# One inference step of a hybrid diffusion layer on one core: the prompt chunk's 128 weighted rows are fetched and summed in another place

## The chip, the core and the metric

The kernel runs on one core of a Trainium2 chip. The core has a matrix engine (TensorE, PE in the profile), VectorE (DVE), ScalarE (ACT), GpSimd (POOL), a queue engine (SyncE, SP) and 16 DMA engines that serve all queues. The metric is the device time of one execution in microseconds, lower is better.

## The reference

Everything is float32. The layer takes 128 prompt tokens and 512 latent tokens (1024 features each) and computes, for both with the same weights: conditioning, normalisation, one input projection, windowed attention with 8 heads, a two-way linear recurrence, an output projection, and then the expert mixer PEER, which this change is about:

```python
def chunk(x):                                   # 128 tokens at a time, 5 chunks: 1 prompt, 4 latent
    q = (x @ w_q).reshape(128, 8, 2, 128)
    s = jnp.einsum('chpd,hpnd->chpn', q, sub_keys)
    st, it = lax.top_k(s, 16)
    cand = st[:, :, 0, :, None] + st[:, :, 1, None, :]
    cidx = it[:, :, 0, :, None] * 128 + it[:, :, 1, None, :]
    best, pos = lax.top_k(cand.reshape(128, 8, -1), 16)
    eidx = take_along_axis(cidx, pos)           # 8 heads x 16 = 128 experts per token
    g = jax.nn.softmax(best, axis=-1)
    act = jax.nn.gelu(einsum('chkd,cd->chk', u_tab[eidx], x))
    return einsum('chk,chkd->cd', g * act, v_tab[eidx])
```

The tables u_tab and v_tab have 16384 rows of 1024 numbers. The result is scaled by a gate, added to x, and x is normalised a last time.

## The kernel before, in words

The five chunks of 128 tokens are called 0 (the prompt), C1, C1+1, C3 and C4 (the latent ones). A token sits on a partition, so that expert slot k of a chunk is one "row": an indirect DMA on POOL's queue fetches, for each of the 128 partitions, the 4 KB row that `eidx[:, c, k]` names, 512 KB in all. A chunk has 128 u rows (each multiplied with x and summed to one dot product) and 128 v rows (each multiplied with a weight of the token, `gw[:, c, k]`, and summed over k).

The program goes through a front for the prompt (phase 0), the same for the latent tokens (phase 1), and then the work on rows.

**The front of phase 1.** The recurrence, then attention in eight quads (4 blocks of tokens times 2 kv heads, each with 4 heads), then the merge: for each of 8 output blocks m a gate product "ga" and an output product "ao" on PE, tanh on ACT, two products on DVE (L1608, L1609), then the output projection "mix" in four token blocks t, each followed by a normalisation on DVE (L1703, L1704) and transposes on PE. PE does the four blocks of mix in order and the transposes of block t after the product of block t+1. Last comes the product with w_q and the top-k of C1.

**The prompt's rows.** Calls `serve(n)` on DVE stand all through the front of phase 1. Each call takes the next n rows of chunk 0: first 128 u rows (L1357), and, once their gelu is done at the end of the recurrence stage (`gelu_dots(0)`), 128 v rows (L1366, one 128x1024 multiply-add into one of two accumulators). They are fetched by POOL into a ring of five buffers. In phase 1 the v rows stand so: 6 a quad in attention (`serve(4)` and `serve(2)`), 16 after it, 6 after each block m of the merge, 8 in each of the first two blocks t of mix; then `add_sums(0)` adds them to x.

**The latent rows.** The list `turns` gives the order in which POOL fetches rows and which engine takes each: step 0 the u rows of C1, step 1 those of C1+1, step 2 those of C3, step 3 the u rows of C4 and the v rows of C3 in turn, step 4 the v rows of C4. The rows share a ring; until step 2 it has 10 buffers (6 until turn 36), and a fetch takes the buffer that has been held longest, so that fetch n waits until row n-10 is used. Turn 36 waits for the end of the w_q product. DVE takes rows with `rows(n)` (L1384), between pieces of the routing of the next chunk: `route(c, piece)` has 12 pieces, eight with two top-k and a top-16 of sums, four that turn positions into expert numbers. `step_end` does the gelu of a chunk's dots.

**The dense chunks.** The v part of C1 and C1+1 is not fetched by rows: the weights are spread into a matrix over all 16384 experts. DVE makes one-hot tiles (`one_hots(i, m)`, L1760 and L1761, 8 instructions for a build of four tokens), PE multiplies them (L946), ACT moves the result (two copies a build), 32 builds for each of the two chunks. The 32 builds of C1 stand in step 1 beside the routing of C3; those of C1+1 follow it. `one_hots` waits for the build two before it (`w_full`). Then the dense product (L959) goes through the whole v table in 128 tiles of 512 KB, loaded by SP into five buffers.

**Summing rows on PE.** Half of the last v rows of C4 are summed by PE: ACT writes a 128x128 diagonal of the row's weights (four buffers), and PE multiplies it with the row, two products of 128x512 accumulated in two PSUM banks (L973; the trace shows four instructions a row).

The profile puts ACT's instructions all at one helper line (L996). DVE's marks go through helper lines too, which is why some waits end at "DVEq L1266".

## Time and profile before

| | us |
|---|---|
| median of 3 runs | 2691.29 (2688.75 to 2694.09) |
| the profiled execution, whole | 2691.56 |
| its span in the profile | 2689.8 |
| PE / DVE / POOL / ACT busy in the span | 1697.5 / 2003.3 / 1044.5 / 352.5 |
| moved by DMA | 753.39 MB, mean 280 GB/s |

All rows below are of the profiled execution. It is 1.8 us longer than its span. A busy share is an average over stages which have different limits, so the rows are mostly read stage by stage.

### The profile page before, as it was taken

How to read it: one execution, taken by the hardware profiler on the slowest of the kernel's cores; microseconds unless marked ns; L12 is line 12 of the kernel's file. 1: busy time of each engine (PE TensorE's matmuls, PEld its weight loads, DVE VectorE, ACT ScalarE, POOL GpSimd, SP SyncE). 2: the span in 40 equal slices, each digit the busy share in tenths (PEclk: the TensorE clock that was granted, in tenths of full speed). 3: DMA queues.
4: the chain of work that ended last, by engine and by line, in shares of the span. 5: the costliest groups of instructions: out<-in, count | busy, mean ns of one | idle time of the engine just before them, and what ended most of it. 6: DMA issues, size and time to landing. Idle time of an engine off the chain costs nothing.

```text
span 2689.8 us, 19725 instructions
## 1 busy us (share of the span) xinstructions
PE 1697.5 (63%) x5821; PEld 1075.7 (40%) x5821; DVE 2003.3 (74%) x4233; ACT 352.5 (13%) x811; POOL 1044.5 (39%) x1028
## 2 busy tenths in 40 slices
PE   6789668989877897794000332069999999000176
PEld 2568543444336545552000222066666666000032
DVE  1331486987679778488999999998876566998845
ACT  0451202541004200111000011020000000000111
POOL 0000002325635556022544343524435445777664
PEclk9899788999988998897555555569999999555588
DMA  9667545658966798263876767849999999999997
GB/s 291 193 203 234 169 151 165 218 180 308 348 203 207 245 374 289 81 219 127 306 283 234 252 224 239 318 157 348 411 410 407 409 409 409 410 370 378 361 373 291
DMA packets 296870, 753.39 MB, mean 280 GB/s; under 512 B 21502, under 2 KB 141102, under 8 KB 296244
## 3 DMA queue, kind: packets, MB, share of 16 engines
q0 software_dynamic: 147456, 536.94, 54.5%
q1 hardware_dynamic: 149308, 215.20, 22.8%
q8 instruction: 47, 0.77, 0.1%
q14 instruction: 59, 0.48, 0.1%
HBM read 740.72 MB, written 11.33 MB: 280 GB/s over the span
## 4 chain that ended last, share of the span: by engine, by line
DVE 41%; issue 26%; PE 16%; DMA 9%; ACT 3%; POOL 2%; DVEq 1%; SPq 0%; ACTq 0%; POOLq 0%
DVE attn L1384 6%; PE bank L724 4%; PE pair L724 4%; DVE big L1384 4%; PE bank L973 3%; DVE ring_more L1384 3%; DVE work L1760 3%; ACT work L996 2%; DMA h_all<-in_peer_u_dram,eidx 2%; DVE gf_row L1761 2%; DMA attn<-in_peer_u_dram,eidx 2%; DMA ring_more<-in_peer_v_dram,eidx 2%; DMA ring_more<-in_peer_u_dram,eidx 2%; PE bank L708 1%; DMA h_all<-in_peer_v_dram,eidx 1%
## 5 line engine op out<-in xcount | busy, mean ns | idle before, releaser
L724 PE MATMUL pair<-big 128*128 128x128 f32 (+1 forms) x1280 | 372.4, 450 | 36.4 <-DVEq L1266 24.9
L1842 POOL DMA_INDIRECT attn<-in_peer_u_dram,eidx x225 | 216.3, 961 | 389.1 <-DVE dots L1384 254.7
L1842 POOL DMA_INDIRECT h_all<-in_peer_u_dram,eidx x106 | 121.1, 1142 | 592.1 <-DVEq L1736 418.3
L724 PE MATMUL bank<-big 128*128 128x512 f32 (+1 forms) x1056 | 313.9, 459 | 37.3 <-DVEq L1270 17.8
L1384 DVE CUSTOM_DVE_ANT_0 attn<-attn,pair 128x1024 f32<-128x1024 f32 x225 | 267.4, 1218 | 45.1 <-DMA attn<-in_peer_u_dram,eidx 28.0
L724 PEld LDWEIGHTS pair<-big 128*128 128x128 f32 x1280 | 203.6, 201 | 192.5 <-issue 176.8
L959 PE MATMUL bank<-h_all,big 128*128 128x512 f32 x608 | 270.3, 601 | 9.9 <-DMA h_all<-in_peer_v_dram 9.2
L1842 POOL DMA_INDIRECT ring_more<-in_peer_u_dram,eidx x161 | 163.8, 1017 | 211.1 <-DVE dots L1384 121.8
L724 PEld LDWEIGHTS bank<-big 128*128 128x128 f32 x1056 | 173.5, 206 | 172.8 <-issue 163.0
L946 PE MATMUL bank<-work,gf_row 128*128 128x128 f32 x512 | 118.9, 409 | 163.4 <-DVE gf_row L1761 163.4
L973 PE MATMUL bank<-big,work 128*128 128x512 f32 x76 | 43.2, 708 | 281.9 <-ACT work L996 264.3
L959 PEld LDWEIGHTS bank<-h_all,big 128*128 128x128 f32 x608 | 180.6, 297 | 95.3 <-DMA h_all<-in_peer_v_dram 10.6
L937 PE MATMUL bank<-ident,sel 128*128 128x128 f32 x4 | 1.3, 439 | 299.5 <-DVEq L1749 299.5
L959 PE MATMUL bank<-big 128*128 128x512 f32 x416 | 182.8, 592 | 0.0
L946 PEld LDWEIGHTS bank<-work,gf_row 128*128 128x128 f32 x512 | 103.5, 300 | 179.1 <-DVE gf_row L1761 178.9
L1842 POOL DMA_INDIRECT big<-in_peer_u_dram,eidx x108 | 104.2, 965 | 109.2 <-DVE dots L1384 79.8
L959 PEld LDWEIGHTS bank<-big 128*128 128x128 f32 x416 | 123.5, 297 | 55.1
L1384 DVE CUSTOM_DVE_ANT_0 ring_more<-ring_more,pair 128x1024 f32<-128x1024 f32 x111 | 132.8, 1217 | 12.7 <-DMA ring_more<-in_peer_u_dram,eidx 8.5
L1842 POOL DMA_INDIRECT h_all<-in_peer_v_dram,eidx x94 | 107.1, 1140 | 85.9 <-DVE gf_row L1366 35.4
L973 PEld LDWEIGHTS bank<-big,work 128*128 128x128 f32 x76 | 16.3, 223 | 305.7 <-issue 305.7
L1384 DVE CUSTOM_DVE_ANT_0 big<-big,pair 128x1024 f32<-128x1024 f32 x108 | 127.4, 1216 | 8.4 <-DMA big<-in_peer_u_dram,eidx 8.1
L1842 POOL DMA_INDIRECT ring_more<-in_peer_v_dram,eidx x87 | 94.7, 1088 | 90.0 <-DVE gf_row L1366 40.4
(255 smaller groups left out, 2966.8 us busy)
## 6 DMA issues: line engine op xcount, KB each, us to landing
big<-in_w_in_dram SPq DMA_DIRECT2D x44, 1024.0 KB, 6.5
h_all<-in_peer_v_dram SPq DMA_DIRECT2D x76, 512.0 KB
big<-in_peer_v_dram SPq DMA_DIRECT2D x52, 512.0 KB
big<-in_w_ada_dram SPq DMA_DIRECT2D x24, 1024.0 KB, 5.5
big<-in_peer_w_q_dram SPq DMA_DIRECT2D x16, 1024.0 KB, 5.5
big<-in_w_rnn_o_dram SPq DMA_DIRECT2D x8, 1024.0 KB, 8.6
big<-in_w_attn_o_dram SPq DMA_DIRECT2D x8, 1024.0 KB, 7.5
big<-in_w_out_dram SPq DMA_DIRECT2D x8, 1024.0 KB, 11.9
```

The source lines that it names most:

```text
L708: last = nc.tensor.matmul(u[0:2, 0:TC], cond[:, k, :], w[:, k, :], start=(k == 0), stop=(k == KD - 1))
L724: last = nc.tensor.matmul(u[:, 0:n], w[:, k, col:col + P], src[:, k, 0:n], start=(k == 0), stop=(k == KD - 1))
L937: last = nc.tensor.transpose(psum[0][:, n * P:(n + 1) * P], src, ident[:, :])
L946: last = nc.tensor.matmul(psum[2 + b % 2][:, t * P:(t + 1) * P], hot_b[at], hot_a[at], start=True, stop=True)
L959: last = nc.tensor.matmul(psum[2 * (c % 2) + h][:, :], dense_w[c][:, q % 2, :, n % QI], v_tile[r][:, h * 512:(h + 1) * 512], start=(n == 0 ...
L973: last = nc.tensor.matmul(psum[i][:, :], diag[:, (n - 1) % DIAGS, :], ring[r][:, i * 512:(i + 1) * 512], start=(k == first_by_tensor), sto ...
L996: return nc.scalar.activation(out, in_, func, **kw)
L1384: V.tensor_tensor_reduce(ring[r], ring[r], x_at[c][:, :], 1.0, 0.0, ALU.mult, ALU.add, dots[:, k:k + 1]).then_inc(row_used["vector"], 1)
L1760: V.tensor_scalar(hot_a[t % HOTS], iota128[:, :], hi[:, t:t + 1], weight[:, t:t + 1], ALU.is_equal, ALU.mult)
L1761: last = V.tensor_scalar(hot_b[t % HOTS], iota128[:, :], lo[:, t:t + 1], None, ALU.is_equal)
L1842: g.indirect_dma_start(dst, None, ins["peer_" + table][0], bass.IndirectOffsetOnAxis(ap=eidx[:, c, k:k + 1], axis=0)).then_inc(landed, 16)
```

## The change

The 128 v rows of chunk 0 leave `serve` and with it the front of phase 1. They become turns of the list: 64 of them stand in step 0 among the u rows of C1 (after the first 36, in the places between 92 u rows), 64 in step 1, one after each two u rows of C1+1. All 128 are summed on PE with diagonals from ACT, into PSUM banks 0 and 1; the transposes of the expert numbers go to bank 2. POOL fetches them through the shared ring. DVE's code for them is gone; a new `add_prompt`, four instructions of 128x512, adds the sum to x in the middle of the builds of C1+1, and the last normalisation of chunk 0 (`final(0)`) follows the last of these builds instead of the end of step 0. On PE the builds of C1 and the weighted rows stand in one order, and so do the diagonals and the moves on ACT. The one-hot tiles use another buffer. The dense product's buffers are dealt out anew: two tiles are loaded ahead instead of three, and the store of chunk 0's result moves behind the load of tile 10.

```diff
     STAGE = 16
     QI = NKEY // 4
-    V_SLOTS, V_FIRST = 5, 3
+    V_SLOTS, V_FIRST = 5, 2
     ALONE = 24
-    turns = [(*step[n % len(step)], n // len(step)) for step in steps for n in range(len(step) * SLOTS)]
-    step_start = [sum(len(step) for step in steps[:i]) * SLOTS for i in range(len(steps))]
+    steps[0] = [("u", C1, k) for k in range(EARLY)]
+    half = SLOTS // 2
+    for k in range(SLOTS - EARLY):
+        n0, n1 = (j * half // (SLOTS - EARLY) for j in (k, k + 1))
+        steps[0] += [("u", C1, EARLY + k)] + [("v", 0, n) for n in range(n0, n1)]
+    steps[1] = []
+    for k in range(half):
+        steps[1] += [("u", C1 + 1, 2 * k), ("u", C1 + 1, 2 * k + 1), ("v", 0, half + k)]
+    steps[2:] = [[(*step[n % len(step)], n // len(step)) for n in range(len(step) * SLOTS)] for step in steps[2:]]
+    turns = [turn for step in steps for turn in step]
+    step_start = [sum(len(step) for step in steps[:i]) for i in range(len(steps))]
+    SOFT_LAG = 22
+    diffs_at = EARLY_ROWS * (2 * PH - 2) + (step_start[1] - EARLY_ROWS * (2 * PH - 2)) * PH // PIECES
+    hots_at = [step_start[1] + len(steps[1]) * PH // PIECES * m // BUILDS for m in range(BUILDS)]
+    later_diffs_at = step_start[1] + len(steps[1]) * PH // PIECES
     taken = {"vector": 0, "tensor": 0}
     by, count_after = [], []
     for table, c, k in turns:
-        by.append("tensor" if table == "v" and c == C4 and k >= ALONE and k % 2 == 0 else "vector")
+        by.append("tensor" if table == "v" and (c == 0 or c == C4 and k >= ALONE and k % 2 == 0) else "vector")
         taken[by[-1]] += 1
         count_after.append(taken[by[-1]])
...
-        acc0 = [gf_row[:, 1, :], final_row[:, :]]
...
-        v_tile = [h2_all[:, C1 + 1, :]] + [big[:, o_h + i * D:o_h + (i + 1) * D] for i in range(2)]
-        v_tile += [h2_all[:, i, :] for i in range(2)]
+        v_tile = [big[:, o_h + i * D:o_h + (i + 1) * D] for i in range(2)] + [h2_all[:, i, :] for i in range(3)]
...
-        hot_b = [gf_row[:, 0, t * P:(t + 1) * P] for t in range(HOTS)]
+        hot_b = [h2_all[:, C1 + 1, t * P:(t + 1) * P] for t in range(HOTS)]
...
-            store(0)
...
-            sp_.wait_ge(x_ready, 2 * len(DENSE))
...
+                if n == 2 * V_SLOTS:
+                    store(0)
...
+            next_row = [0]
+            def weighted_rows(end):
+                for turn in range(next_row[0], end):
+                    table, c, k = turns[turn]
+                    if by[turn] != "tensor":
+                        continue
+                    r, n = slot_of[turn], count_after[turn]
+                    pe.wait_ge(diag_ready, n)
+                    pe.wait_ge(row_in[r], landings[turn])
+                    for i in range(2):
+                        last = nc.tensor.matmul(psum[i][:, :], diag[:, (n - 1) % DIAGS, :],
+                                                ring[r][:, i * 512:(i + 1) * 512], start=(k == first_by_tensor[c]),
+                                                stop=(k == last_by_tensor[c]))
+                    last.then_inc(row_used["tensor"], 1)
+                next_row[0] = max(next_row[0], end)
...
+            def turn_ids(i):
                 pe.wait_ge(ids_split, i + 1)
...
+            weighted_rows(step_start[1])
+            turn_ids(0)
+            for m in range(BUILDS):
+                weighted_rows(hots_at[m])
+                weights(0, m)
+            weighted_rows(step_start[2])
+            pe.drain().then_inc(sums_full, 1)
+            pe.wait_ge(w_moved, BUILDS)
+            turn_ids(1)
+            for m in range(BUILDS):
+                weights(1, m)
+            pe.wait_ge(sums_free, 1)
...
-            pe.wait_ge(sums_free, 1)
...
+            pe.wait_ge(sums_free, 2)
+            weighted_rows(len(turns))
...
             soft(C1)
             spread_x(C1 + 1)
+            diags(diffs_at + SOFT_LAG)
             soft(C1 + 1)
+            diags(step_start[1])
             gelu_dots(C1)
-            final(0)
             spread_x(C3)
             spread_ids(0)
-            move_weights(0)
+            for m in range(BUILDS):
+                diags(hots_at[m])
+                move_weights(0, m)
+            diags(later_diffs_at + SOFT_LAG)
             soft(C3)
+            diags(step_start[2])
             gelu_dots(C1 + 1)
...
+            for m in range(BUILDS):
+                move_weights(1, m)
+            final(0)
...
-                    if s_ is None or s_ == 2 * SLOTS or (s_ == SLOTS and not gelu0[0]):
+                    if s_ is None or s_ == SLOTS:
...
-                    if s_ < SLOTS:
-                        V.tensor_tensor_reduce(ring0[r], ring0[r], h2_all[:, 0, :], 1.0, 0.0, ALU.mult, ALU.add,
-                                               dots[:, s_:s_ + 1]).then_inc(slot0_used, 1)
-                    else:
-                        a_, w_ = acc0[s_ % 2], gw[:, 0, s_ - SLOTS:s_ - SLOTS + 1]
-                        if s_ < SLOTS + 2:
-                            V.tensor_scalar(a_, ring0[r], w_, None, ALU.mult).then_inc(slot0_used, 1)
-                        else:
-                            dve.wait_ge(slot0_used, RING0 + s_ - 1)
-                            V.scalar_tensor_tensor(a_, ring0[r], w_, a_, ALU.mult, ALU.add).then_inc(slot0_used, 1)
+                    V.tensor_tensor_reduce(ring0[r], ring0[r], h2_all[:, 0, :], 1.0, 0.0, ALU.mult, ALU.add,
+                                           dots[:, s_:s_ + 1]).then_inc(slot0_used, 1)
...
                     if ph and t == 1:
-                        serve(2 * SLOTS)
-                        dve.wait_ge(slot0_used, RING0 + 2 * SLOTS)
-                        dve.wait_ge(final_in, 16)
-                        add_sums(0, acc0)
                         dve.drain().then_inc(sums0_done, 1)
...
+                    dve.wait_ge(x_ready, 2 * len(DENSE))
...
+            def add_prompt():
+                dve.wait_ge(sums_full, 1)
+                for i, h in enumerate([slice(i * 512, (i + 1) * 512) for i in range(2)]):
+                    link(V.tensor_tensor(psum[i][:, :], psum[i][:, :], gf_row[:, 0, h], ALU.mult))
+                    link(V.tensor_tensor(x_all[:, 0, h], x_all[:, 0, h], psum[i][:, :], ALU.add))
+                dve.drain().then_inc(sums_free, 1)
...
-            left = SLOTS - next_turn[0]
+            left = step_start[1] - next_turn[0]
             for piece in range(PIECES):
                 route(C1 + 1, piece)
                 rows(share(left, piece, PIECES))
             step_end(C1)
-            dve.wait_ge(final_in, 48)
-            final(0, hot[:, 0:D])
             split_ids(C1)
             for piece in range(PIECES):
                 route(C3, piece)
-                n_rows, n_hots = share(SLOTS, piece, PIECES), share(BUILDS, piece, PH) if piece < PH else 0
-                for m in range(n_hots):
-                    one_hots(0, BUILDS * piece // PH + m)
-                    rows(share(n_rows, m, n_hots))
-                if not n_hots:
-                    rows(n_rows)
+                for m in range(BUILDS * piece // PH, BUILDS * (piece + 1) // PH if piece < PH else 0):
+                    rows(hots_at[m] - next_turn[0])
+                    one_hots(0, m)
+                if piece >= PH:
+                    rows(max(later_diffs_at - next_turn[0], 0))
+                    rows(share(step_start[2] - later_diffs_at, piece - PH, PIECES - PH))
             step_end(C1 + 1)
             split_ids(C1 + 1)
             for m in range(BUILDS):
                 one_hots(1, m)
                 rows(m % 2)
+                if m == BUILDS // 2:
+                    add_prompt()
+            dve.wait_ge(final_in, 48)
+            final(0, hot[:, 0:D])
...
-            for n in range(2 * SLOTS):
+            for n in range(SLOTS):
                 r = n % RING0
                 pool.wait_ge(slot0_used, n + 1)
-                fetch("u" if n < SLOTS else "v", 0, n % SLOTS, ring0[r], row0_in[r])
-            pool.wait_ge(slot0_used, RING0 + 2 * SLOTS)
+                fetch("u", 0, n, ring0[r], row0_in[r])
+            pool.wait_ge(slot0_used, RING0 + SLOTS)
```

## Rows read from the trace of the kernel before

**Rows 1.** Busy time by stage: from:to, length, engines, granted PE clock, DMA share, GB/s
```profile
796.90:914.30 117.40, 87.10 (x502) 72.48 (x501) 101.91 (x133) 42.66 (x110) 55.26 (x46) 0.86 0.60 207
914.30:1036.40 122.10, 104.04 (x248) 46.03 (x246) 86.33 (x77) 7.25 (x11) 66.00 (x60) 0.95 0.92 334
1264.20:1455.30 191.10, 0.00 (x0) 0.00 (x0) 184.25 (x452) 0.43 (x2) 96.90 (x103) 0.50 0.77 276
1468.70:1669.10 200.40, 66.45 (x256) 57.03 (x256) 196.87 (x603) 22.02 (x65) 78.91 (x84) 0.50 0.69 232
1669.10:1747.70 78.60, 0.90 (x3) 0.50 (x3) 73.26 (x143) 1.86 (x7) 39.59 (x41) 0.50 0.85 307
1747.70:1824.20 76.50, 51.44 (x253) 45.74 (x254) 76.46 (x289) 20.41 (x63) 14.89 (x15) 0.70 0.51 162
1825.90:2280.10 454.20, 444.93 (x1024) 304.02 (x1024) 323.82 (x621) 1.95 (x6) 203.96 (x216) 0.99 1.02 406
1284.00:1300.00 16.00, 0.00 (x0) 0.00 (x0) 15.48 (x44) 0.00 (x0) 9.72 (x11) 0.50 1.03 414
```

**Rows 2.** The same by stage for line L1366 alone (DVE busy, clock, DMA)
```profile
796.90:914.30 117.40, 54.18 (x44) 0.86 0.60 207
914.30:1036.40 122.10, 75.31 (x60) 0.95 0.92 334
```

**Rows 3.** One attention quad: all engines' busy time, then PE and ACT instructions
```profile
816.60:831.60 15.00, 9.26 (x64) 8.63 (x63) 13.84 (x19) 5.90 (x14) 7.33 (x7) 0.81 0.61 217
831.60:845.40 13.80, 10.57 (x70) 9.83 (x70) 12.64 (x18) 5.25 (x14) 7.19 (x7) 0.87 0.64 220
...
828.98 1.97 PE L864 MATMUL pair<-ident,work 128*128 128x128 f32 x8 [5.74 <-DVEq L1266]
...
822.86 0.20 ACT L996 ACTIVATE q_es<-q_dif 128x4 f32<-128x4 f32 x1 [3.89 <-DVEq L1652]
```

**Rows 4.** PE in merge and mix (start, length, [idle before, releaser]); DVE's last merge
```profile
990.97 27.63 PE L724 MATMUL pair<-big 128*128 128x512 f32 x64
1036.44 30.17 PE L898 MATMUL bank<-big 128*128 128x256 f32 x128 [17.84 <-DVEq L1611]
...
1088.72 1.97 PE L890 MATMUL pair<-ident,h_all 128*128 128x128 f32 x8 [7.43 <-DVE h_all L1704]
...
1035.55 0.69 DVE L1609 TENSOR_TENSOR big<-big,work 128x512 f32<-128x512 f32 x1
```

**Rows 5.** A fetch and a product of u rows, POOL and DVE
```profile
1277.05 0.94 POOL L1842 DMA_INDIRECT big<-in_peer_u_dram,eidx  x1 [0.30 <-issue]
...
1453.87 1.22 DVE L1384 CUSTOM_DVE_ANT_0 big<-big,pair 128x1024 f32<-128x1024 f32 x1
```

**Rows 6.** Chain of waits: a u row on its way, start and length
```profile
1149.58 4.87 DMA attn<-in_peer_u_dram,eidx
```

**Rows 7.** A fetch beside one-hot tiles, POOL and DVE
```profile
1508.90 0.94 POOL L1842 DMA_INDIRECT ring_more<-in_peer_u_dram,eidx  x1 [0.30 <-issue]
...
1508.81 0.35 DVE L1760 TENSOR_SCALAR work<-vcols,attn 128x128 f32<-128x128 f32 x1
```

**Rows 8.** PE: weighted rows (four instructions each), then builds (eight each)
```profile
2554.00 1.88 PE L973 MATMUL bank<-h_all,work 128*128 128x512 f32 x4
...
2573.47 3.63 PE L973 MATMUL bank<-big,work 128*128 128x512 f32 x4 [2.15 <-issue]
...
1510.31 2.08 PE L946 MATMUL bank<-work,gf_row 128*128 128x128 f32 x8 [3.17 <-DVE gf_row L1761]
...
1797.46 1.16 PE L946 MATMUL bank<-work,gf_row 128*128 128x128 f32 x8 [1.81 <-DVE gf_row L1761]
```

**Rows 9.** ACT: one of a build's two moves
```profile
1507.18 0.38 ACT L996 ACTIVATE big<-bank 128x256 f32<-128x256 f32 x1 [4.60 <-PE bank L946]
```

**Rows 10.** DVE: first and last large instruction of final(0)
```profile
1457.01 1.23 DVE L1276 CUSTOM_DVE_ANT_0 work<-x_all 128x1024 f32<-128x1024 f32 x1 [0.18 <-DVE gw L1412]
...
1459.72 1.28 DVE L1426 SCALAR_TENSOR_TENSOR x_all<-x_all,nrm,final_row 128x1024 f32<-128x1024 f32 x1
```

80 lines of the change are left out of this document (33 added, 47 removed).

## The prediction

> **What bounds the kernel now.** I read the busy time by stage first, because 74% of busy DVE over the whole span says nothing of one stage. Four regimes are to be seen. In attention and merge of phase 1 DVE has most to do, 101.9 of 117.4 us, and then waits for rows, 86.3 of 122.1 us while the DMA share is 0.92 [rows 1]. In step 0 (1264 to 1455) and step 1 (1469 to 1748) DVE is busy 184.3 of 191.1, 196.9 of 200.4 and 73.3 of 78.6 us, with the DMA engines at 0.77, 0.69 and 0.85, PE at 0.50 of its clock and nearly idle [rows 1]. In the dense product PE is busy 444.9 of 454.2 us and the DMA engines are at 1.02, 406 GB/s [rows 1]. So the change takes work from a stretch that is bound by DVE and by its rows, and puts its fetches where DVE binds and the DMA engines have room; the room is what has to be counted. Second I read the line of the weighted rows by stage: 54.2 us of DVE in attention and 75.3 us up to the start of mix [rows 2]. Third the waits inside one quad, in merge and in mix.
>
> **The front.** 128 products of some 1.28 us leave DVE. What that is worth is the distance to what binds next.
> Attention: a quad takes 15.0 or 13.8 us, of which six v rows fill 7.4 to 7.7. PE then waits 5.74 us for a mark of DVE, ACT 3.89 us for the maxima [rows 3]. With the rows gone PE comes next: it is busy 9.3 and 10.6 us in the two quads [rows 3]. I take 10.0 us for a quad: 14.4 - 10.0 = 4.4, times 8 = 35 us, less 1 for the two ends, **-34**. Bounds: if only the row time that PE and ACT both wait for goes (3.9 of each quad in part, say 2) it is -16; if all of six rows goes, 7.5 x 8 = -60, which PE's busy time excludes below 9 us a quad, so -43.
> Merge and mix: PE ends its last merge products at 1018.6 (990.97 + 27.63) and starts mix at 1036.44, after 17.84 us of waiting for DVE's last merge, which ends at 1036.24 [rows 4]. Without six rows a block DVE needs two products of 0.7 us after PE's last one, so some 2 us stay: -16. In mix PE waits 7.43 us for the normalisation of block 1, behind `add_sums` and eight rows [rows 4]; without them DVE needs about 9.5 us a block where PE needs 15 (30.17 for two), so all of it goes: -7. Together **-23**. Here PE's own work cannot shrink, which makes this the surest term. The u part of chunk 0 stands before all this and stays. Front: -57.
>
> **Step 0.** DVE's own work stays at 191 us (rows of u, routing). The fetches grow: turns 38 to 191 are issued in it, 154 instead of 90, because ten are in the ring when the routing part before it ends. A fetch costs POOL 0.94 + 0.30 = 1.24 us back to back [rows 5]. In the stretch with fetches alone the DMA engines are at 1.03 and move 414 GB/s, that is 0.524 MB / 414 = 1.27 us a row [rows 1]. So 1.27 binds: the first issue comes with the first product at 1271, the last u row (turn 190) is issued 152 x 1.27 = 193 us later, at 1464, lands in 4.9 us [rows 6], more under load, say 6, and is multiplied in 1.22 [rows 5]: 1471 against 1455, +16. The queue is in order and a ring of 10 is short: in the 6 us of a routing piece 5 fetches fit, and 5 are on their way, so it holds just, and a v row keeps its buffer until ACT's diagonal and PE's product. I add 0.5 us in each of 12 pieces: **+22**. Bounds: 154 x 1.24 hidden up to landing, +8; 1.5 us a turn, 154 x 1.5 = 231, +47.
>
> **Step 1, beside the builds.** 16 turns a piece of 25.7 us (8 pieces, 206 us), 20.3 us of DMA: room. New is the order on PE and ACT: rows, build, two moves, the next diagonals, rows. A weighted row takes PE 1.88 us at the full clock and 3.63 after a pause of 2.15 us [rows 8], a build 1.16 or 2.08 [rows 8], the moves 2 x 0.38 [rows 9], diagonal and marks some 0.5. With 4/3 rows a build the cycle is 4.9 us at 2.4 GHz and 8.2 at 1.2 GHz, and DVE offers 206/32 = 6.4 and may lead by two builds only. In the builds of C1+1, PE is busy 67% of the time and granted 0.70 [rows 1]; the new mixture would be busy longer than that, so I take the same 0.70 at least: (1.16 + 2.5)/0.70 + 1.3 = 6.5 us, a tie, **+6** for bursts. Bounds 0 and (8.2 - 6.4) x 32 = +58.
> **Step 1, last four pieces**: 64 turns x 1.27 = 81 us against 73 of DVE work there; the ring is full at the start, which gives back part: **+5** (0 to +10).
> `final(0)` leaves the end of step 0: 1457.0 to 1461.0, **-4** [rows 10]. `step_end` waits for u rows alone; the last v row is 2 to 4 us later on PE and hidden by gelu, split and the first routing piece.
>
> **Builds of C1+1 and after.** DVE is busy 76.46 of 76.50 us there [rows 1], so `add_prompt` counts: four of 128x512, nearest row 0.69 [rows 4], with marks **+3**. `final(0)` comes after the last build, beside the dense product, where DVE has 130 us idle: 0 to +2. The third tile is no longer loaded ahead: two tiles last 2 x 3.5 us (454/128), a tile needs 4.9 or more [rows 6] from the last save on: +2. The store of chunk 0 (0.5 MB) now falls where the DMA engines are full: 0.524/406 = +1.3. Together **+4**. From here the fetches, their order and the bytes are those of before, and at 1.02 DMA share the rest moves as a whole.
>
> **Sum.** -34 - 23 + 22 + 6 + 5 - 4 + 3 + 4 = -21 us on the profiled execution's 2691.56 (span 2689.8 plus 1.8), which is 0.3 above the median shown: 2670.
>
> **Two rules of the Trainium skill against this.** A fetch beside one-hot tiles takes POOL 0.94 us, as any other, and the next follows after 0.30 [rows 7]. "SBUF — State Buffer", section "SBUF: two separate sides", says that a VectorE tensor_scalar can hold the port by which GpSimd writes its descriptors. By that rule the one-hots would shut POOL out for 8 x 0.3 us a build, and four fetches would need 5.0 + 2.4 = 7.4 us a build where 6.4 are there, +32; the trace does not show it, and I give it 3 in 100 (rival 4).
> After 2.15 us without work PE's next row is at the lower level [rows 8], and PE sits at 0.50 with 33% of busy time in step 1 today [rows 1]. "TensorE: Matmul & The Clock Gate", section "HAM oscillation — how this bites in real kernels", describes loops that wait for a DMA between short bursts and fall back each time. By that rule rows of both steps would start low; in step 0 this is harmless, a row every 3 x 1.27 = 3.8 us against 3.63; in step 1 it is rival 3.
>
> **Rivals.**
> 1. The room is there (20 in 100). Fetches run ahead, step 0 costs +8, step 1 nothing: -57 + 8 - 4 + 3 + 4 = -46, 2646. For it: DMA shares of 0.69 to 0.85. Against: 82 MB in step 0 at 414 GB/s is 198 us, more than DVE's 191.
> 2. The front gives less (13 in 100). ACT's exponentials and copies, which wait for PE in turn, make the quad 12.5 us instead of 10: -20 more away, 2690. For it: the three engines hand over some 20 times a quad; against: ACT is busy only 5.9 us [rows 3].
> 3. **Slower**: the chain of rows, build, moves and diagonals sets step 1 (14 in 100). PE stays at 1.2 GHz in it, 8.2 us a build, +58 instead of +6: -21 + 52 = +31, 2722. It decides from where a build takes 6.4 + (6 + 21)/32 = 7.2 us: above that the kernel is slower. For it: 0.50 through today's step 1. Against: the same builds, put closer, are granted 0.70.
> 4. Fetches slow down as such (5 in 100, the rule on the port among it): at 1.5 us a turn in both steps 25 more in step 0 and about 15 more in step 1, or the +32 above: 2702 to 2710.
> The case that the change does not do what it says is small: the v rows are gone from the code of the front, so their 128 products must go.
>
> **From this the numbers.** The forecast has 48 in 100, with its own range 2656 to 2684. A measurement of this kernel tells 0.2%, 5.4 us, from no change. Faster by more: nearly all of the forecast, rival 1 and a quarter of rival 2, 0.72. Within: 0.10. Slower: rivals 3 and 4 and the edge of the others, 0.18. The range of 8 in 10 reaches from rival 1 (2646, less 4 for its own spread) to short of rival 3: 2642 to 2704.
>
> **What would show it.** In the changed profile: no 128x1024 multiply-add of chunk 0 between 800 and 1080; quads of about 10 us; no wait ahead of the first mix product; the w_q product starting near 1057 instead of 1114. Step 0 (first routing piece of C1+1 to the last u row of C1) of 213 us with a DMA share near 1.0 and DVE waiting for DMA rows; the builds of C1 at 6.6 us each with a clock between 0.6 and 0.8; the dense product again 454 us long. I am wrong if step 0 stays at 191, if a quad stays above 12, or if a build takes over 7.2 us.

## The result and the profile after

In the first comparison, that of the profiled pair, the changed kernel took 2719.4 us (2718.5 to 2732.4) against 2692.7 (2688.8 to 2696.8): ratio 1.0109, interval 1.009 to 1.0128. Forecast was 2670, so the sign is wrong. Repeated on three chips it was slower each time: 1.0101 [1.0073, 1.0128], 1.0086 [1.0051, 1.0121] and 1.0113 [1.0084, 1.0141]. On two further chips only variants of it ran; on one of them the same code with twelve buffers took 0.993 [0.991, 0.995] (one of its four executions was slow, 3044.6 us at a granted clock of 0.639, and is left out). What differs there is the main finding.

Busy time by stage of the changed kernel (from:to, length, engines, granted TensorE clock, DMA share, GB/s), to be laid beside [rows 1]; the front first, then step 0 from its first product, the builds of C1, the last four routing pieces, the builds of C1+1, the dense product:

```profile
797.00:877.00 80.00, 76.13 (x495) 63.16 (x494) 45.50 (x84) 43.29 (x111) 0.00 (x0) 0.98 0.00 1
877.00:974.00 97.00, 96.74 (x229) 42.98 (x228) 9.67 (x14) 6.66 (x10) 0.00 (x0) 1.00 0.29 98
...
1201.70:1435.80 234.10, 139.01 (x252) 48.80 (x252) 181.01 (x427) 23.74 (x61) 151.80 (x160) 0.88 0.93 354
1445.30:1657.10 211.80, 126.41 (x397) 68.52 (x398) 195.27 (x597) 31.30 (x100) 110.62 (x117) 0.81 0.85 316
1657.10:1760.70 103.60, 62.10 (x119) 22.12 (x118) 78.49 (x149) 11.71 (x34) 70.70 (x73) 0.86 0.97 372
1760.70:1840.20 79.50, 51.77 (x255) 46.01 (x256) 79.25 (x293) 20.41 (x62) 14.93 (x15) 0.70 0.52 163
1842.50:2296.70 454.20, 444.99 (x1024) 303.64 (x1022) 324.50 (x630) 3.72 (x8) 201.45 (x213) 0.99 1.02 405
```

The kernel before in three of these stretches:

```profile
797.00:877.00 80.00, 59.48 (x352) 51.30 (x351) 72.44 (x97) 31.14 (x81) 35.64 (x30) 0.86 0.56 192
877.00:974.00 97.00, 86.96 (x294) 47.80 (x294) 71.27 (x74) 15.11 (x35) 53.49 (x46) 0.95 0.80 282
...
1270.60:1455.10 184.50, 0.00 (x0) 0.00 (x0) 178.34 (x427) 0.31 (x1) 96.70 (x103) 0.50 0.79 282
```

The front is as hoped: PE is busy 96.74 of 97 us where it had waited. In step 0 DVE does the same work (181.0 against 178.3 us busy) in 234.1 us instead of 184.5. The rest of PE's timeline of the front (start, length, [idle before, releaser]), against [rows 4]:

```profile
950.12 27.63 PE L735 MATMUL pair<-big 128*128 128x512 f32 x64
979.47 27.89 PE L909 MATMUL bank<-big 128*128 128x256 f32 x128 [1.72 <-DVEq L1642]
...
1043.18 1.97 PE L901 MATMUL pair<-ident,h_all 128*128 128x128 f32 x8 [5.56 <-DVE h_all L1731]
1045.87 4.64 PE L735 MATMUL pair<-big 128*128 128x512 f32 x5 [0.72 <-ACTq L1023]
```

The last merge product ends at 977.8 against 1018.6 before; the wait ahead of mix is 1.72 instead of 17.84 us; the w_q product starts at 1045.9 instead of 1114.5. That is 68.6 us won. 97 us are lost behind it, and the span is 28.4 longer. What DVE waited for in step 0 (us in total, times, longest):

```profile
DVE attn L1416 <- DMA attn<-in_peer_u_dram,eidx: 12.1, 10, 1.9
DVE big L1416 <- DMA big<-in_peer_u_dram,eidx: 9.3, 8, 2.0
DVE big L1521 <- remote: 6.7, 2, 3.7
DVE ring_more L1416 <- DMA ring_more<-in_peer_u_dram,eidx: 4.9, 3, 2.2
...
DVE work L1471 <- remote: 1.9, 1, 1.9
```

26.3 us are waits for rows, which the forecast had in mind. The others are of a kind it had not: L1521 and L1471 are inside a routing piece, where each instruction waits for the mark of DVE's own last one alone (the semaphore that it raises at its end), and "remote" says that the trace names no releaser. The timeline at one such place, all engines:

```profile
1257.39 0.29 DVE L1520 MAX8 big<-big 128x8 f32<-128x128 f32 x1
1257.41 0.94 POOL L1880 DMA_INDIRECT ring_more<-in_peer_v_dram,eidx  x1 [0.75 <-remote]
...
1258.92 1.96 PE L956 MATMUL bank<-attn,work 128*128 128x512 f32 x4 [1.89 <-DMA attn<-in_peer_v_dram,eidx]
...
1260.68 0.40 ACT L1028 ACTIVATE work<-ident,gw 128x128 f32<-128x128 f32 x1 [8.72 <-remote]
1260.92 0.94 POOL L1880 DMA_INDIRECT ring_more<-in_peer_u_dram,eidx  x1 [2.56 <-remote]
1261.38 0.09 DVE L1521 MATCH_VALUE_LOAD big<-big 128x8 f32 x1 [3.71 <-remote]
```

DVE's MAX8 ends at 1257.68, and its next instruction starts 3.71 us later; the mark it waits for is recorded at 1261.36, right ahead of its start. PE does a whole row in between, and ACT and POOL start when that row is done, so those two waited for PE. What stands still without a reason in sight is DVE. I call such a wait a stop, and count as stops DVE's waits of over 0.5 us that the trace puts down to none of DMA, PE, ACT and POOL. In step 0 they add up to 18.8 us here and to 0.0 in the kernel before. Of the 18.8 us, 15.7 are inside routing pieces; 3.1 stand ahead of products of rows, where the count may take in a wait for a row.

### The profile page after: what moved, and what is told of

Its sections match the earlier page's. It is cut to its first block, busy times and chain, and to the rows that moved or that the text cites. A ratio compares the mean times of both kernels' runs of the same rounds, so it can differ in the third digit from the quotient of the medians.

```text
span 2718.2 us, 20760 instructions
## 1 busy us (share of the span) xinstructions
PE 1944.3 (72%) x6333; PEld 1147.1 (42%) x6333; DVE 1851.9 (68%) x4106; ACT 398.1 (15%) x939; POOL 1016.0 (37%) x1028
## 4 chain that ended last, share of the span: by engine, by line
DVE 31%; PE 25%; DMA 19%; issue 11%; POOL 8%; ACT 4%; another core or an unknown queue 2%; SPq 0%; DVEq 0%; ACTq 0%; PEldq 0%; PEld 0%; POOLq 0%
DMA attn<-in_peer_u_dram,eidx 6%; PE pair L735 6%; PE bank L735 6%; PE bank L956 4%; DVE attn L1416 4%; DMA ring_more<-in_peer_u_dram,eidx 3%; DMA attn<-in_peer_v_dram,eidx 3%; PE bank L909 3%; POOL big L1880 2%; ACT work L1028 2%; POOL attn L1880 2%; DMA h_all<-in_peer_u_dram,eidx 2%; DVE big L1428 2%; DVE ring_more L1416 2%
## 5 line engine op out<-in xcount | busy, mean ns | idle before, releaser
L956 PE MATMUL bank<-big,work 128*128 128x512 f32 x272 | 155.9, 707 | 402.3 <-ACT work L1028 302.8
L735 PE MATMUL bank<-big 128*128 128x512 f32 (+1 forms) x1056 | 310.7, 455 | 32.0 <-DVEq L1312 17.8
L956 PEld LDWEIGHTS bank<-big,work 128*128 128x128 f32 x272 | 55.2, 219 | 489.2 <-issue 454.7
L956 PE MATMUL bank<-attn,work 128*128 128x512 f32 x260 | 144.0, 686 | 82.6 <-DMA attn<-in_peer_v_dram,eidx 44.4
L1416 DVE CUSTOM_DVE_ANT_0 big<-big,pair 128x1024 f32<-128x1024 f32 x111 | 133.0, 1218 | 31.6 <-DMA big<-in_peer_u_dram,eidx 27.3
L1880 POOL DMA_INDIRECT attn<-in_peer_v_dram,eidx x122 | 117.7, 965 | 56.0 <-issue 30.6
L1880 POOL DMA_INDIRECT big<-in_peer_v_dram,eidx x111 | 108.8, 980 | 69.3 <-issue 27.8
L976 PE MATMUL bank<-work,h_all 128*128 128x128 f32 x512 | 91.2, 338 | 51.7 <-DVE h_all L1789 38.7
L1028 ACT ACTIVATE work<-ident,gw 128x128 f32<-128x128 f32 x180 | 69.1, 400 | 389.1 <-PE bank L956 182.0
```

Of the source, the lines that this page charges most:

```text
L735: last = nc.tensor.matmul(u[:, 0:n], w[:, k, col:col + P], src[:, k, 0:n], start=(k == 0), stop=(k == KD - 1))
L956: last = nc.tensor.matmul(psum[i][:, :], diag[:, (n - 1) % DIAGS, :], ring[r][:, i * 512:(i + 1) * 512], start=(k == first_by_tensor[c]), ...
L976: last = nc.tensor.matmul(psum[2 + b % 2][:, t * P:(t + 1) * P], hot_b[at], hot_a[at], start=True, stop=True)
L1028: return nc.scalar.activation(out, in_, func, **kw)
L1416: V.tensor_tensor_reduce(ring[r], ring[r], x_at[c][:, :], 1.0, 0.0, ALU.mult, ALU.add, dots[:, k:k + 1]).then_inc(row_used["vector"], 1)
L1880: g.indirect_dma_start(dst, None, ins["peer_" + table][0], bass.IndirectOffsetOnAxis(ap=eidx[:, c, k:k + 1], axis=0)).then_inc(landed, 16)
```

## Experiments

Times are compared on one chip only, stages of traces without stops also across chips (step 0 without weighted rows takes 184.5 us in the kernel before on A and 184.4 on B). B to F are five different chips. A is the first comparison; the number of its chip is not on record, so it may be one of C, D and F. All runs of one chip were made at one time. A "v row" is a weighted row of the prompt chunk.

**Chip B** (before: 2668.5 us). Leave the v rows out, all or step 0's:

```
-  steps[0] += [("u", C1, EARLY + k)] + [("v", 0, n) for n in range(n0, n1)]
+  steps[0] += [("u", C1, EARLY + k)]
-  steps[1] += [..., ("v", 0, half + k)]          (e1 only)
```

> The changed kernel with the 128 v rows of the prompt chunk left out altogether (that part of the prompt's sum is missing). It gives the price of their new place by difference. Theory A (the fetches of the added rows, through a ring of ten buffers, stretch steps 0 and 1): the front stays 69 us shorter, step 0 (first routing piece of C1+1 to the last u row of C1) falls from 240 to about 191 us, the stretch beside the builds from 212 to about 200, the last four pieces from 104 to about 79: 2719 - 49 - 12 - 25 = 2633, and if the 12 us that the stretch after the dense product has lost go too, 2621. Theory B (what got longer is the new order on PE and ACT, with or without rows): the builds stay at 212 us, 2645 or more. Theory C (the front's gain is not what its start times say): above 2660.

Measured 2602.3 us, 0.9757 [0.9741, 0.9773]. Step 0 takes 184.4 us from its first product, the builds 196.6, the last four pieces 82.5. That is under the whole time expected, and so is the next run: the expectations were reckoned from chip A.

> The changed kernel with the 64 v rows of step 0 left out (half of the prompt's sum is missing); the 64 of step 1 stay. Theory A: only step 0 gets back its 49 us: 2719 - 49 = 2670, step 1 unchanged at 212 and 104 us. If the load of step 0 reaches into step 1 (a full ring handed over late), step 1 gets shorter too: 2660.

Measured 2625.1, 0.9842 [0.9825, 0.9858]; step 0 184.9, builds 202.6, last four pieces 97.6. So step 1's 64 rows cost 6 us among the builds and 15 in the last four pieces.

Two buffers more in step 0 (its ring of ten gets `h2_all[:, 0:2]`):

```
+  if turn < step_start[1] - 12:
+      return [*range(10), RING, RING + 1]
...
```

> The changed kernel with a ring of 12 buffers instead of 10 in step 0 (two free buffers of h2 added). Nothing left out. In the trace POOL waits 30 us in step 0 for DVE to give a buffer back, while DVE waits 26 us for rows. If the short ring is the cause of the 49 us (theory A, ring), two more fetches are under way in each of the 12 routing pieces, 2 x 1.27 = 2.5 us each, so step 0 falls by 20 to 30 us: about 2694. If the DMA engines' rate is (theory A, rate: 154 turns x 1.27 = 196 us plus the ends), at most 10 us. If the stalls in DVE's routing pieces, about 20 us that no row shows as a wait for data, are the cause, no change: 2715 to 2719.

Measured 2649.4, 0.993 [0.991, 0.995]: no clean answer, as the kernel was below every number expected. Half the product of each v row (`for i in range(2 if c else 1)` in `weighted_rows`):

> The changed kernel with only the first of a prompt row's two products on PE (the right half of the prompt's sum is missing); every fetch, diagonal and wait stays. The prediction's rival 3 (the chain of rows, build, moves, diagonals on PE and ACT sets step 1): the builds of C1 get 4/3 x 0.9 to 1.8 us shorter each, 32 x 1.7 = up to 50 us, in any case the whole 12 us of step 1 that were lost beside the builds: 2705 or less. Theory A (fetches): PE is not waited for, no change within 3 us: 2716 to 2722.

Measured 2648.4, 0.9917 [0.9898, 0.9936]. Busy time in step 0, first of the twelve buffers, then of the half product:

```profile
1200.50:1411.30 210.80, 126.41 (x252) 44.05 (x252) 180.73 (x427) 24.28 (x61) 153.01 (x162) 0.95 1.00 395
```

```profile
1205.80:1417.40 211.60, 124.56 (x126) 30.80 (x126) 180.81 (x427) 24.28 (x61) 154.27 (x162) 0.53 1.00 394
```

Two quite different edits give 211 us each, at a granted clock of 0.95 and 0.53, where chip A had 234. The stops are 0.0 in both traces, and a routing piece of two top-k takes 6.3 us, as in the kernel before, where on chip A five of the seven between products of step 0 take 9.3 to 12.2. That two such edits should do the same was unlikely, which made the chip the suspect.

**Chip C** (before: 2688.6). The changed kernel again:

> The changed kernel itself, beside the variants and beside the kernel before on the same chip. In the first comparison it stood at 1.011 of the kernel before, but two variants that should not have been far from it (twelve buffers; one product a row in place of two) stood at 0.992 and 0.993 on another chip, with step 0 at 211 us from its first product, against 234 us in the profiled run of the changed kernel, and with routing pieces of 6.3 us against 6.4 to 12. Theory S (the long routing pieces, some 24 us of step 0 and 12 us behind the dense product, belong to the execution or the chip and not to the change): ratio 0.990 to 0.997, step 0 209 to 213 us, last four pieces 95 to 98. Theory R (the ring: twelve buffers gave 24 us of step 0): ratio 1.005 to 1.015, step 0 232 to 236. Theory P (the second product of a row gave them): the same 1.005 to 1.015, with the ring variant no better than chance.

Measured 2714.5, 1.0101 [1.0073, 1.0128], step 0 233.1, stops 18.6. So the loss comes back, with its stops, and does not belong to one execution. The v fetches with half the bytes:

```
+  table_, dst = (ins["peer_v"][0].rearrange("n (a d) -> (n a) d", a=2), dst[:, 0:512]) if table == "v" and c == 0 else ...
```

> The fetches of the prompt chunk's weighted rows bring 2 KB a partition in place of 4 KB (the second half of such a row in the ring stays what it was, so the prompt's sums are wrong); their number, order and buffers are unchanged. Theory A (bytes: step 0 is held by the DMA engines at 380 to 395 GB/s): step 0 moves (90 + 32)/154 of the bytes and is then held by VectorE as before, 185 to 190 us in place of 210; the last four pieces 82 to 88 us in place of 95 to 98; 25 to 35 us less than the changed kernel. Theory R (a fixed time from a buffer's release to its next landing, ring too short) or a price of GpSimd for every fetch (1.24 us each, 154 = 191 us): step 0 falls by under 10 us.

Measured 2724.1, 1.0129 [1.0097, 1.0162]. Not a microsecond is won: step 0 236.0, stops 26.1, though the DMA share is down.

```profile
1199.50:1435.50 236.00, 144.25 (x253) 51.77 (x254) 180.92 (x427) 22.87 (x61) 153.02 (x162) 0.84 0.82 282
```

Half the v rows back in the front, behind the `u` part of `serve`, in merge and mix alone; the other 64 in step 1 as they were:

```
+  FRONT, IN0 = 64, 0                     (rows in the front, in step 0)
-  serve(16)                              (behind the attention)
+  serve(14 if ph else 16)
-  serve(8 if a == "gr" else 6)           (merge)
+  serve(8 if a == "gr" else [7, 7, 7, 7, 3, 3, 3, 3][m] if ph else 6)
-  serve(4) ... serve(2)                  (in a quad)
+  serve(0 if ph else 4) ... serve(0 if ph else 2)
-  serve(2)                               (mix; the last two follow after block 1)
+  serve(1 if ph else 2)
...
```

> 64 of the prompt's 128 weighted rows are taken by VectorE in the front's merge and mix blocks (none in the attention), the other 64 by TensorE in step 1, none in step 0. Theory A: of the front's 69 us 32 to 38 are given back, step 0 falls to 185 us (-25), step 1 stays: 2 to 12 us slower than the changed kernel and 5 to 15 faster than the kernel before. Rival (the front has room for 64 rows, since VectorE waits there for the merge and mix weights): under 20 us given back, and it is the fastest of all.

Measured 2668.5, 0.9919 [0.9892, 0.9946]; step 0 184.8 with stops 0.0, but 8.6 us of stops in the last four pieces, which take 107.0 us. The front below. And step 1's 64 v rows all among the builds (149 turns there, later_diffs_at and hots_at moved with them):

> Step 1's 64 weighted rows of the prompt chunk all go among the 32 one-hot builds (149 turns there, of them 85 product rows as in the changed kernel), none in the last four pieces. Theory A (each fetch costs its 1.36 us of the DMA engines, and the builds have room for 20 more in 200 us): last four pieces 79 to 83 us in place of 95 to 98, builds 200 to 208 in place of 199 to 203: 8 to 18 us faster than the changed kernel. Rival (TensorE and ScalarE set the builds: a weighted row more a build is late for them): builds 215 or more, no faster than the changed kernel.

Measured 2718.0, 1.0099 [1.0061, 1.0136]. Against the changed kernel on this chip the last four pieces fall from 101.0 to 85.5 and the builds rise from 211.7 to 237.5: nothing is won, as the rival had it.

**Chip D** (before: 2687.8). The two edits of chip B and the changed kernel together:

> Twelve ring buffers in step 0, once more, now on one chip with the changed kernel: on a first chip it had 0.993 of the kernel before, and on a second chip the changed kernel had 1.010. Theory C (the two chips differ: on the one, all engines stand still together for 1 to 4 us at a time while the DMA engines are full, on the other not; the ring does nothing): within 0.3 per cent of the changed kernel on this chip, whichever value that has, and both of one kind: 0.992 to 0.996 with no such stops in the routing pieces, or 1.008 to 1.015 with them. Theory R (the ring of ten): 20 us or more faster than the changed kernel here too.

> One of the two 512-column products of a prompt row left out (half of the prompt's sums missing), once more on one chip with the changed kernel. Theory C (as for the ring of twelve): within 0.3 per cent of the changed kernel on this chip. Theory P (TensorE's second product holds a buffer and the chain of weighted rows): 20 us or more faster than the changed kernel, and step 0 at 210 to 213 us against its 232 to 236. Theory W (the stops come with TensorE's work beside full DMA traffic, which the half product halves): the stops are gone in it and not in the changed kernel.

> The changed kernel on the same chip as the two variants. Theory C: of one kind with them, 0.992 to 0.996 without stops or 1.008 to 1.015 with them. Theories R, P and W: 1.008 to 1.015 while the variant concerned stands at 0.992 to 0.996.

Measured 1.0122 [1.0084, 1.016], 1.011 [1.0073, 1.0147] and 1.0086 [1.0051, 1.0121]: one kind, within 0.4% of each other. Step 0 took 235.0, 242.0 and 229.0 us, with stops of 28.0, 34.5 and 14.2. Neither ring nor product brings the 20 us that theories R and P ask for. The half product again, same code as on chip B, with 30 us more:

```profile
1201.10:1443.10 242.00, 128.63 (x126) 31.55 (x126) 180.41 (x427) 24.28 (x61) 152.94 (x162) 0.51 0.89 343
```

DVE, PE, ACT and POOL are busy about as long as on chip B (180.8, 124.6, 24.3, 154.3), and the DMA engines move 343 GB/s and not 394. DVE's idle time ahead of products of rows is 23.6 us against 25.2, ahead of its other instructions 33.8 against 0.3: all of the 30 us is lost inside the routing. Theory C had one thing wrong, that all engines stand still together. One of the stops of the kernel with twelve buffers on this chip:

```profile
1313.42 0.28 DVE L1525 MATCH_REPLACE8 work<-big 128x128 f32<-128x128 f32 x1
1313.93 0.94 POOL L1883 DMA_INDIRECT attn<-in_peer_u_dram,eidx  x1 [0.30 <-issue]
...
1315.17 0.94 POOL L1883 DMA_INDIRECT ring_more<-in_peer_v_dram,eidx  x1 [0.30 <-issue]
...
1316.42 0.94 POOL L1883 DMA_INDIRECT ring_more<-in_peer_u_dram,eidx  x1 [0.30 <-issue]
...
1317.48 0.29 DVE L1526 MAX8 big<-work 128x8 f32<-128x128 f32 x1 [3.79 <-remote]
```

DVE waits 3.79 us for its own last instruction, and POOL issues one fetch after the other. In the eight traces with stops and 154 turns DVE has 95 stops inside routing pieces; in 76 of them, and in all 40 over 1.2 us, PE, ACT or POOL start an instruction.

80 rows in the front (two in each of eight quads besides), 48 in step 1:

> 80 of the weighted rows by VectorE in the front (two of them in each attention quad... 16 in all there, the others in the merge and mix blocks), 48 by TensorE in step 1, none in step 0. The kernel with 64 in the merge and mix blocks started its row products within 3 us of the changed kernel, so these 64 cost the front next to nothing, and had 0.992. If the front has room for 16 more: 5 to 8 us less than that kernel, by 16 fetches fewer in the crowded last four pieces. If the attention has no room, as in the kernel before (its rows set the quads at 12.7 us against 10): 8 to 12 us more in the front and 5 to 8 less in step 1, within 0.3 per cent of the kernel with 64.

Measured 2662.9, 0.9889 [0.9848, 0.9929], the front 4 us later than with 64 (first product of step 0 at 1209.5 against 1205.4).

**Chip E** (before: 2665.2; again one without stops). 512 bytes a partition (`a=8`, `dst[:, 0:128]`):

> The fetches of the prompt chunk's weighted rows bring 512 bytes a partition in place of 4 KB (the rest of such a row in the ring stays what it was, so the prompt's sums are wrong); number, order and buffers unchanged. Half the bytes left step 0 at 236 us with 26 us of stops at a DMA share of 0.82. Theory F (stops come with GpSimd's fetches issued without a pause, whatever they bring): stops of 10 us or more in step 0, step 0 at 205 to 225 from its first product, time within 10 us of the changed kernel's. Theory B (they come with the DMA engines' load): no stops, step 0 at 190 to 195 us (154 turns of 1.24 us), the time 30 to 50 us under the changed kernel's 1.010.

Measured 2639.6, 0.99 [0.9883, 0.9916]. Stops 0.0, but all kernels of this chip have none, so theories F and B are not told apart. Another thing is: step 0 is 205.0 us, not 190 to 195. POOL's fetches and the time ahead of them there:

```profile
L1881 POOL DMA_INDIRECT big<-in_peer_u_dram,eidx x40 | 38.1, 953 | 12.7 <-issue 11.0 <-DVE dots L1416 1.7
L1881 POOL DMA_INDIRECT attn<-in_peer_u_dram,eidx x37 | 34.9, 944 | 11.3 <-issue 10.4 <-DVE dots L1416 0.9
L1881 POOL DMA_INDIRECT attn<-in_peer_v_dram,eidx x27 | 25.8, 955 | 8.2 <-issue 7.0 <-PE bank L956 0.9 <-DVE dots L1416 0.3
L1881 POOL DMA_INDIRECT big<-in_peer_v_dram,eidx x24 | 23.0, 960 | 7.3 <-issue 4.6 <-PE bank L956 2.4 <-DVE dots L1416 0.3
```

It issues 162 fetches at 0.95 + 0.30 us, 202 us in 205, with no long pause but one of 8.9 us that begins ahead of the stretch: with the bytes gone GpSimd binds. 32 rows in step 0, 64 in the front, 32 in step 1 (`FRONT, IN0 = 64, 32`):

> 64 weighted rows in the front, 32 by TensorE in step 0, 32 in step 1. Step 0 then has 122 turns. At the rate of the chip without stops (1.37 us a turn) 167 us are asked of the fetches, under VectorE's 185: step 0 stays at 185 to 187 us and the last four pieces lose half of their 17 to 20 us; 8 to 12 us under the kernel with 64 and none (0.992). Theory T (stops in proportion to the weighted rows among the products): half of the changed kernel's 14 to 19 us of stops, step 0 at 195 to 200, and the time equal to that of the kernel with 64 and none within 5 us.

Measured 2610.1, 0.9793 [0.9777, 0.9809], the fastest complete kernel, and further below the kernel with 64 and none than expected (that one's 0.992 is of a chip with stops). Its stages: 877 to 974, step 0, builds, last four pieces.

```profile
877.00:974.00 97.00, 96.74 (x229) 42.98 (x228) 68.89 (x63) 6.66 (x10) 54.82 (x48) 1.00 0.95 349
...
1201.00:1387.50 186.50, 97.58 (x128) 31.19 (x128) 179.14 (x427) 11.44 (x29) 124.81 (x131) 0.72 0.96 361
1397.00:1593.70 196.70, 105.37 (x325) 64.26 (x326) 193.28 (x596) 26.16 (x82) 93.28 (x99) 0.69 0.78 280
1593.70:1678.40 84.70, 43.66 (x63) 14.66 (x61) 77.15 (x151) 6.46 (x20) 56.54 (x58) 0.68 0.99 380
```

Step 0, builds and last pieces are within 2.2 us each of the kernel without any v row (184.4, 196.6, 82.5). Two more splits, with step 1's rows all among the builds:

> As the kernel with 80 rows in the front (0.989), but the 48 rows of step 1 all go among the 32 builds (133 turns there), none in the last four pieces. If the fetches among the builds have room for 16 more: last four pieces 80 to 84 us in place of 97, builds 202 to 206: 10 to 14 us less, 0.984 to 0.986. If they go as with 64 rows there (builds 237 us, last four 85): builds 212 to 218, no gain.

> 96 rows in the front (four in each attention quad, 32 there), 32 in step 1, all among the builds (117 turns there, as many as in the changed kernel's). If two rows more a quad are nearly free (the first two cost the front 3 us in all): front +3, builds 198 to 202, last four pieces 80 to 84: 15 to 20 us under the kernel with 80, 0.982 to 0.985. If each row in a quad now costs its 1.28 us: front +20, equal to the kernel with 80 rows.

Measured 2628.8, 0.9862 [0.9846, 0.9879] and 2630.4, 0.9856 [0.9831, 0.988]. With 48 rows the builds take 211.2 us (133 turns), so little is gained there; with 32 they take 197.9, but four rows a quad cost the front 27 us (first product of step 0 at 1227.7 against 1201.0 in the kernel with none in the quads).

**Chip F** (before: 2695.6; with stops).

> The changed kernel. Theory C (stops of all engines on some chips and not on others, whatever the variant): where the kernel before takes 2660 to 2670 us, 0.992 to 0.995, with no stops and step 0 at 209 to 213 us from its first product (GpSimd's 162 fetches there at 1.245 us are 202); where the kernel before takes 2680 to 2700, 1.008 to 1.012 with 14 us of stops or more in step 0. Rival (one of the variants' edits mattered on the chips without stops): over 1.000 where the kernel before takes 2660 to 2670.

> 64 weighted rows in the front, 32 in step 0, 32 in step 1, once more. Theory C: 0.977 to 0.982 where the kernel before takes 2660 to 2670 us. Where it takes 2680 to 2700: stops come in step 0 with the 32 rows, 5 to 10 us of them, and in the last four pieces, and the ratio is 0.982 to 0.988; below the kernels with 64 and none (0.992) and with 80 and none (0.989) if the stops grow more slowly than the rows.

Measured 2726.8, 1.0113 [1.0084, 1.0141], step 0 234.6 with stops of 20.2; and 2653.2, 0.9856 [0.9829, 0.9883], step 0 191.0 with stops of 4.0, a little under the 5 to 10 expected. The split 64/32/32 beats the kernel before on either kind of chip, 2610 against 2665 and 2653 against 2696, and the changed kernel on this one.

## Why the prediction was wrong

Microseconds against the kernel before; the column "without stops" is the run with twelve buffers on chip B, its stages laid against those of before on chip A, which had no stops up to the dense product.

| term | forecast | chip A | without stops |
|---|---|---|---|
| attention | -34 | -41 | about the same |
| merge wait, mix | -23 | -28 | about the same |
| step 0 | +22 | +50 | +26 |
| final(0) leaves | -4 | -4 | -4 |
| builds of C1 | +6 | +11 | +2 |
| last four pieces | +5 | +25 | +19 |
| C1+1's builds up to the first row after them | +7 with the next | +8 | +9 |
| behind that | | +7 | not separable |
| sum | -21 | +28 | -17 (ratio 0.993, -19) |

**The front was right in its mechanism, and 12 us small.** A quad: PE does 495 products in 80 us against 352, so 14.4 x 352/495 = 10.2 us, forecast 10.0. The wait of 17.84 us fell to 1.72 as forecast. Mix takes 66.4 us against 78.0, forecast -7. But the sum priced the 128 rows as one, and they are not alike. Of the 80 rows that stood behind the last quad, the kernel of e14 keeps 64 (14 ahead of the merge, 7 after each of its first four blocks and 3 after the others, 10 in mix). DVE is busy 68.9 instead of 9.7 us between 877 and 974, PE is busy 96.74 of 97 in both, and the w_q product starts at 1045.0 in it against 1045.9:

```profile
978.64 27.89 PE L913 MATMUL bank<-big 128*128 128x256 f32 x128 [2.19 <-DVEq L1656]
...
1045.04 11.18 PE L739 MATMUL pair<-big 128*128 128x512 f32 x20 [0.72 <-ACTq L1027]
```

So PE's products can cover these 64; the change moved them out for nothing and paid for them in steps 0 and 1. My text says that PE's own work cannot shrink there, but not the next sentence: then so many rows are free.

**The failed step is step 0: "DVE's own work stays at 191 us" and "So 1.27 binds", +22 with +47 as its bound.** It cost 50 us on chip A. Two things are in it. Where there are no stops, the term held: 26 for 22. The DMA engines moved 395 and not 414 GB/s (210.8 us x 395 GB/s / 0.524 MB = 159 rows of 1.33 us), and where DVE waited for a row, it had it 5.3 us after the end of POOL's issuing instruction in the half product's trace (the mean over the rows waited for, the n-th u fetch against the n-th u product), forecast 6. With twelve buffers that was 6.8, at the same rate: a longer ring in front of full DMA engines is a longer queue. On the other chips step 0 cost 44 to 58 us in eight traces, with 14 to 35 us of stops, 8 to 33 of them inside routing pieces. On chip A DVE is idle for 30.8 us ahead of products of rows and for 17.8 ahead of its other instructions; with twelve buffers on B these are 24.5 and 0.3. The sum had added DVE's routing as a fixed time and charged all the rest to the fetches' rate; that DVE could wait for its own last instruction no term, bound or rival had. I had read the stretch [rows 1] with its DMA share of 1.03 as the state in which step 0 would run, and it was only 16 us long. None of the signs by which I would have called myself wrong came (step 0 at 191, a quad above 12, a build above 7.2 us): they did not cover this. One sum in rival 1 is off too: 154 rows of 0.524 MB are 80.7 MB, 195 us and not 198.

**Last four pieces: "64 turns x 1.27 = 81 us" was mis-sized.** The stretch takes 97.2 us without stops: 393 GB/s, that is 73 rows, not 64, at 1.33 us. The rows are those that make the ring full again behind the builds; I had counted the ring as a gain ("full at the start"), and it is nearly empty there: at the start of the stretch the changed kernel on A has issued the fetches of 318 turns, and 316 turns stand ahead of the last build.

**Builds: right on the mechanism.** 211.8/32 = 6.6 us each at 0.81, as forecast; without stops 6.3 at 0.82. Rival 3 did not come, and the row after 1.89 us without work above takes 1.96 us, not 3.63. Step 0 of e3 and e4, with PE at 0.95 and at 0.53, differs by 0.8 us (they differ in the ring too). The Trainium skill's "TensorE: Matmul & The Clock Gate", section "HAM oscillation — how this bites in real kernels", describes loops of short bursts and waits that fall back to the lower level; the trace agrees (0.53 with one 512-column product a row), but in this stretch it costs nothing. The rule of the Trainium skill's "SBUF — State Buffer", section "SBUF: two separate sides", by which a tensor_scalar can hold GpSimd's port, is not borne out: 117 fetches beside the one-hots took 110.62 us, 0.95 each, as elsewhere. But beyond 117 turns there the builds grow by 0.8 us for each: from 197.9 to 211.2 with 133 on chip E, from 211.7 to 237.5 with 149 on C. POOL waits 44 us in that stretch for PE's release of v rows in the trace with twelve buffers, so the order on PE is likelier the limit than the DMA engines, with a share of 0.89; no run tells the two apart.

**Behind the dense product: +7.** From the first row after the builds to the end the kernel before takes 859.3 us on chip A, the changed one 866.5, 863.1, 862.0 and 869.0 on A, C, D and F, and on B and E eight kernels take 836.5 to 838.2 each. In the kernel before, too, DVE has stops there (36.1 us, 15.2 of them not at products of rows), and none in steps 0 and 1. The kernel before has no trace on B or E; if it is like the others there, it loses by my estimate some 22 us on A behind its last build, about what lies between its 2688 to 2696 us and its 2665 to 2668. GB/s in 40 slices of the changed kernel on A, then of the one with twelve buffers on B; the last six figures stand behind the dense product:

```profile
GB/s 291 188 212 237 161 138 177 219 182 330 344 115 8 101 47 114 211 176 345 352 379 320 330 313 330 366 154 348 411 409 409 409 409 409 409 378 386 313 374 278
```

```profile
GB/s 286 205 187 225 175 181 159 206 190 278 355 216 1 75 84 64 207 127 344 409 410 328 334 341 353 393 158 321 409 410 411 409 410 409 409 410 410 377 386 314
```

The dense product is the same 409 in both, fed by SP's transfers beside POOL's; what follows it, fed by POOL's fetches, moves 358 GB/s on A and 384 on B.

**Near the forecast by luck.** Without stops the sum comes within 4 us of -21, but the terms do not: the front gave 12 us more, and the last four pieces cost 14 us more, step 0 four more and the builds four less.

**What is shown and what is open.** Shown: DVE waits for its own late marks in all twelve traces of A, C, D and F behind the front, and in none of the eight of B and E. In step 0 stops come in every kernel with 154 turns (eight traces, 14 to 35 us), little with 122 (4.0 us), not with 90 (three traces); two of those three have 9 us of them in the last four pieces. They are not due to the ring, to the second product, or to the bytes of the v rows as far as halving them tells. Not told apart: on these chips 154 turns always came with weighted rows on PE and ACT beside them. Not shown: why DVE's own mark is late, and whether that lies in the chip or in what else went on beside it at the time.

One more rival stands untested: the recording. The twelve traces with stops lack marks. Two lines of `--dma` in step 0, of the half product on B and of the changed kernel on A; the second gives no time to landing, because landing marks are missing:

```profile
big<-in_peer_u_dram,eidx POOLq DMA_INDIRECT x40, 6.5
```

```profile
big<-in_peer_u_dram,eidx POOLq DMA_INDIRECT x40
```

The trace of the changed kernel on A has 13248 of the 21408 landing marks that its transfers should leave, that of the kernel before 16813, that with twelve buffers on B 21261. Of the engines' own marks in step 0 the changed kernel's trace has 182 of 393, the one with twelve buffers all 393. Of these 182, 41 are recorded late. In 80 of the 95 stops inside routing pieces a late mark of DVE's is recorded within 0.12 us of the restart, and marks of other instructions are missing within 2 us of all 95; the latter says little, as they are missing over some three quarters of step 0. So what makes marks go missing in the record may also be what holds DVE back, and then part of the loss would belong to the recording. Every timed execution here has a recorded span and clock, so no run tells how the kernels stand to each other unrecorded on such a chip.

"Runtime: NRT & Kernel Launch" of the Trainium skill, section "Instruction fetch mechanics", says that engines fetch their instructions by DMA in blocks of 16 KiB, which would be a candidate. In chip A's step 0 there were nine such transfers, two of 16 KiB and seven of 8, none in the 4 us ahead of the end of any of DVE's four waits marked remote, and the trace with twelve buffers on B has nine as well and no stop, so the traces do not speak for it. The changed kernel itself was never timed on a chip without stops; by its variants e3 and e4 I estimate it near 0.993 there, 2 us from the forecast.

## What to carry to other kernels

Price work that is to be moved in pieces, by what covers each piece where it stands: 64 of these rows fit under TensorE's merge and mix products for nothing, and the front's whole gain of 69 us was in taking out the other 64, 1.1 us each. Do not fill a queue to its rate for a long stretch: 32 rows added to step 0's 90 turns cost it 2 us without stops and 6 with them, 64 cost 26 and 44 to 58. And when two edits that have nothing in common give the same surprise, run the unedited kernel beside them on the same chip before explaining either. A releaser that the profile calls remote, in a kernel on one core, is a reason to count the marks in the trace.

## What the runs showed of the hardware

- In twelve traces, of A, C, D and F, VectorE at times waits up to 5.0 us in step 0 (e10) for the mark of its own last instruction, while TensorE and GpSimd go on (40 of 40 waits over 1.2 us); in 80 of 95 cases a late mark is in the record. The kernel before takes 2688 to 2696 us there. In the eight traces of chips B and E, where it takes 2665 to 2668 us, there is no such wait. The traces of the first kind lack marks: 13248 of 21408 landing marks are in the changed kernel's on A, 21261 in e3's on B.
- GpSimd issues an indirect fetch every 1.25 us whether it brings 4 KB or 512 bytes a partition; the DMA engines carry 4 KB rows at 1.33 us (395 GB/s) next to row work. With half the bytes in the v rows their busy share fell only from 0.95 to 0.82, while the rate went from 357 to 282 GB/s.
- With one 512-column product a row TensorE was granted 0.51 to 0.53 in step 0, with two and full rows 0.86 to 0.95; on chip B step 0 took 211.6 and 210.8 us with them.
